# Per-head sums in the projection loop of a four-layer block kernel: four 64x64 products on the four quadrants of TensorE in place of two full products

## The reference, cut to what matters

```python
r, k, v, g, w_lo, a_lo = jnp.split(h, list(np.cumsum(widths)[:-1]), axis=-1)
a = jax.nn.sigmoid(a0 + a_lo @ a2)
...
kk = (k * k_k).astype(jnp.float32)
kk = kk / jnp.maximum(jnp.linalg.norm(kk, axis=-1, keepdims=True), 1e-12)
k = k * (1 + (a - 1) * k_a)
...
bonus = (jnp.sum(r * k * r_k, axis=-1, keepdims=True) * v).reshape(B, L, D_INNER)
```

## Time and profile before

| what | us |
|---|---|
| median of 3 runs (2550.43 to 2552.8) | 2550.72 |
| the profiled execution's own time | 2552.2 |
| its span | 2549.9 |
| TensorE busy | 2213.5 (87%) |
| VectorE busy | 1401.9 (55%) |
| GpSimd busy | 1207.3 (47%) |
| ScalarE busy | 824.4 (32%) |
| mean granted TensorE clock | 0.925 of full speed |

### The profile page before, as it was taken

The page is one execution under the profiler, slowest core; times in us unless marked ns, Lnnn a source line. Parts: engine busy times, 40 slices in busy tenths (PEclk is TensorE's granted clock), DMA queues, the critical chain, the costliest instruction groups (busy, mean ns, idle before and its releaser), DMA issues.

```text
span 2549.9 us, 56210 instructions
## 1 busy us (share of the span) xinstructions
PE 2213.5 (87%) x22038; PEld 1868.7 (73%) x22038; DVE 1401.9 (55%) x2028; ACT 824.4 (32%) x2139; POOL 1207.3 (47%) x708
## 2 busy tenths in 40 slices
PE   6799999988888989886867999999894999798876
PEld 4699989877777878775867976777694776565555
DVE  6766666666666566664445413445415172638655
ACT  1532233325545555453212222333201111211331
POOL 1366656633223132233855831222384897775134
PEclk8899999999988889896987999999897999899998
DMA  2233344372333233323211221000022221221001
GB/s 86 85 141 141 153 150 151 136 196 44 81 62 71 58 71 74 69 48 109 79 64 50 83 74 34 33 33 23 27 83 94 74 91 42 66 83 58 17 0 66
DMA packets 158904, 197.54 MB, mean 77 GB/s; under 512 B 120992, under 2 KB 123296, under 8 KB 156448
## 3 DMA queue, kind: packets, MB, share of 16 engines
q1 hardware_dynamic: 158752, 195.25, 25.2%
HBM read 156.24 MB, written 38.99 MB: 77 GB/s over the span
## 4 chain that ended last, share of the span: by engine, by line
PE 56%; DVE 11%; issue 5%; ACT 4%; POOL 1%; DVEq 1%; ACTq 0%; POOLq 0%
PE wide L797 9%; PE wide L1224 8%; PE wide L1225 8%; PE wide L1226 8%; PE wide L1701 4%; PE wide L1810 2%; PE wide L812 2%; PE wide L820 1%; PE wide L1586 1%; PE wide L1766 1%; DVE x_w L1022 1%; PE wide L814 1%; DVE b_and_k L1015 1%; PE wide L1794 1%; PE wide L2063 1%
## 5 line engine op out<-in xcount | busy, mean ns | idle before, releaser
L1077 POOL TENSOR_TENSOR n_levels<-n,masks 128x192 f32<-128x192 f32 (+1 forms) x96 | 117.8, 1239 | 437.5 <-ACT n L958 437.5
L1224 PE MATMUL wide<-mixed_high,w_high_rwkv_in 128*128 128x264 f32 x720 | 213.0, 296 | 27.8 <-ACT log_decay L435 18.9
L1226 PE MATMUL wide<-mixed_high,w_low_rwkv_in 128*128 128x264 f32 x720 | 207.5, 288 | 0.0
L1341 DVE TENSOR_TENSOR sq_sum<-sq_sum,squares 128x528 f32<-128x528 f32 (+1 forms) x54 | 87.3, 1617 | 178.6 <-ACT squares L1306 178.6
L1225 PE MATMUL wide<-u_low_second,w_high 128*128 128x512 f32 x464 | 185.5, 400 | 0.0
L1248 POOL TENSOR_TENSOR w_high<-weights,con 128x1024 fp32r<-128x1024 f32 x60 | 147.5, 2459 | 73.6 <-PE wide L1226 63.7
L355 PE MATMUL wide<-mixed_in,weights 128*128 128x264 f32 x672 | 158.7, 394 | 13.7 <-DVE mixed_in L325 12.3
L1224 PEld LDWEIGHTS wide<-mixed_high,w_high_rwkv_in 128*128 128x128 f32 x720 | 139.0, 193 | 36.2 <-ACT log_decay L435 25.1
L1251 POOL TENSOR_TENSOR w_low<-weights,w_high 128x1024 fp32r<-128x1024 f32 x60 | 157.6, 2627 | 4.7
L355 PEld LDWEIGHTS wide<-mixed_in,weights 128*128 128x128 f32 x672 | 128.9, 193 | 41.0 <-issue 9.5
L797 PE MATMUL wide<-x_w,n_levels 64*64 64x64 f32 x2752 | 121.8, 231 | 37.8 <-DVE x_w L1022 21.0
(11 more groups left out here) (325 smaller groups left out, 6495.0 us busy)
## 6 DMA issues: line engine op xcount, KB each, us to landing
weights<-in_stream SPq DMA_DIRECT2D x200, 512.0 KB, 3.3
forms<-form SPq DMA_DIRECT2D x16, 2020.5 KB, 6.3
forms_in<-forms SPq DMA_DIRECT2D x96, 144.0 KB, 4.5
forms_in<-forms SPq DMA_DIRECT2D x32, 288.0 KB, 4.5
gate_bonus<-forms SPq DMA_DIRECT2D x16, 576.0 KB, 4.0
r_ahat_r<-forms SPq DMA_DIRECT2D x32, 144.0 KB, 3.1
mixed<-gate_bonus SPq DMA_DIRECT2D x14, 264.0 KB, 2.1
gated<-mixed SPq DMA_DIRECT2D x14, 264.0 KB, 4.8
```

The source lines that it names most:

```text
L1077: return pool.tensor_tensor(n_lvl[:, first:last, grp(g), :], n_all[:, grp(g), :].unsqueeze(1).to_broadcast([P, n, GC, C]), b_con[:, 1 + fi ...
L1224: pe.matmul(dst, w[0], x[0], start=start, stop=False)
L1226: return pe.matmul(dst, w[1], x[0], start=False, stop=stop)
```

## The change

Each sum is made by four products instead of two. Product (head, b) reads the head's 64 rows of half b and writes 64 rows of bank b: for b = 0 the head's own rows, for b = 1 the other head's rows. Each of the four so has its own quadrant of the array. The two readers, ScalarE's square root (line 446) and VectorE's bonus product (line 518), become three instructions each: one for the first half on all 128 partitions, and one per head for the second half, which reads the other head's rows of PSUM and writes the head's rows of SBUF. Ahead of each sum TensorE increments a semaphore `sums_turn` that nobody waits for, so that its waits are taken there, and the two products of head 0 increment `sums_first`, which the readers wait for in addition.

```diff
+        TWO = (slice(0, C), slice(C, P))
+
+        def head_sums(pe, dst, src):
+
+            pe.sem_inc(s["sums_turn"], 1)
+            for hd, rows in enumerate(TWO):
+                for b in range(2):
+                    mm = pe.matmul(dst[TWO[hd ^ b], b, 0:HALF], heads[rows, hd * C:(hd + 1) * C], src[rows, PAD + b * HALF:PAD + (b + 1) * HALF],
+                                   start=True, stop=True)
+                    if hd == 0:
+                        mm.then_inc(s["sums_first"], 1)
+            return mm
+
+        def summed_parts(src):
+
+            cols = [slice(PAD + b * HALF, PAD + (b + 1) * HALF) for b in range(2)]
+            return [(slice(0, P), cols[0], src[:, 0, 0:HALF])] + [(TWO[hd], cols[1], src[TWO[1 - hd], 1, 0:HALF]) for hd in range(2)]
...
             pe.wait_ge(s["k_copied"], i + 1)
             pe.wait_ge(s["kk_squared"], i + 1)
-            for b in range(2):
-                mm = pe.matmul(wide[2][:, b, 0:HALF], heads, a_sq[:, PAD + b * HALF:PAD + (b + 1) * HALF], start=True, stop=True)
-            mm.then_inc(s["kk_summed"], 1)
+            head_sums(pe, wide[2], a_sq).then_inc(s["kk_summed"], 1)
...
-            for b in range(2):
-                mm = pe.matmul(wide[3][:, b, 0:HALF], heads, a_rk[:, PAD + b * HALF:PAD + (b + 1) * HALF], start=True, stop=True)
-            mm.then_inc(s["rk_summed"], 1)
+            head_sums(pe, wide[3], a_rk).then_inc(s["rk_summed"], 1)
...
             act.wait_ge(s["kk_summed"], i + 1)
-            act.activation(real(a_inv), wide[2][:, :, 0:HALF], ACT.Sqrt).then_inc(s["kk_rooted"], 1)
+            act.wait_ge(s["sums_first"], 4 * i + 2)
+            for rows, cols, part in summed_parts(wide[2]):
+                ins = act.activation(a_inv[rows, cols], part, ACT.Sqrt)
+            ins.then_inc(s["kk_rooted"], 1)
...
             dve.wait_ge(s["rk_summed"], i + 1)
-            step(dve.tensor_tensor(real(f_bon), wide[3][:, :, 0:HALF], real(f_v), ALU.mult))
+            dve.wait_ge(s["sums_first"], 4 * i + 4)
+            for rows, cols, part in summed_parts(wide[3]):
+                ins = dve.tensor_tensor(f_bon[rows, cols], part, f_v[rows, cols], ALU.mult)
+            step(ins)
```

More of the change, by code:

```diff
@@ L278, in program @@
             "diff", "lerp", "lora_loaded", "lora_low", "proj_w", "proj_a", "tanh_w", "tanh_a", "k_copied", "r_copied", "kk_squared",
-            "p_exp", "kk_summed", "kk_rooted", "v_copied", "g_tanh", "pc_copied", "rk_summed", "dve", "pool", "stored", "in_rounded", "in_rest", "in_whole")}
+            "p_exp", "kk_summed", "kk_rooted", "v_copied", "g_tanh", "pc_copied", "rk_summed", "dve", "pool", "stored", "in_rounded", "in_rest", "in_whole", "sums_first", "sums_turn")}
         def half_bias(n, pair):
```

## The result

| | changed | before, same chip |
|---|---|---|
| median of the runs | 2575.18 us (2573.42 to 2576.63) | 2551.76 us (2550.43 to 2553.3) |
| ratio | 1.0091, interval 1.0074 to 1.0109 | |
| profiled execution | 2574.58 us, span 2572.8 | 2552.2 us, span 2549.9 |

The change costs 0.9%, 23.4 us of the medians. The forecast was 2556.0 with a range to 2565.5. Both are missed, on the side that rival A was on.

A forecast was written before the change was run, and what follows sets the result against it. TensorE bounds the pair with VectorE 0.18 us behind; VectorE's +0.43 overtakes it. Pairs 3 to 15, 3.1, pair 2, 0.4, pair 0, 1.0, end, 0.8: +5.3 us, 2556.0 against the 2550.72 median; range 2552.0 to 2565.5.

The forecast's parts named there:

- rival A: VectorE's line 500 comes after GpSimd's line 534 and waits it out: +0.91 us per pair, 2565.2 us in all, chance 0.18.
- ScalarE's part: Square root of the sum in three instructions takes 0.95 us in place of 0.61: +0.34, bounds +0.2 to +0.6.
- the point of decision: ScalarE delay, over 0.55 us in place of the forecast 0.34, at which VectorE's line 500 must wait out GpSimd's line 534.
- VectorE's part: Bonus product in three instructions, one every 0.35 us, against 0.62 before: +0.43, bounds +0.3 and +0.6.
- what would show it: The prediction's list of signs in the trace, among them line 500 over 2 us long in all pairs for rival A.
- the slot: Time for VectorE's line 500 ahead of GpSimd's line 534; missing it ends VectorE's chain 0.67 us later than forecast.
- entry and exit as priced: TensorE's cost of changing from the full array to quadrants and back, per sum: 0.15 us in, 0.20 us out.
- The slack of 0.18: Per pair, how far VectorE's chain, ending at line 521, could slip before TensorE's receptance projection is delayed: 0.18 us.
- the 0.21 us to the weight load: Time from the end of VectorE's line 521 to the receptance projection's first weight load: 0.21 us, between 0 and 0.25.
- The gap between two GpSimd instructions: VectorE's line 500 runs between GpSimd's lines 531 and 534; issued at 275.08, before 275.29, it hides ScalarE's 0.34 us.
- The ends: Loop's first and last pairs: pair 0 +0.98 us, line 500 locked out by GpSimd; last chain +0.77 us, both delays counting.
- the forecast's premise: In the readers' three parts, each instruction overlaps the one before, starting 0.10 us before its end on ScalarE.

The follow-up runs named there:

- both_overlapping: Kernel before with both readers in three instructions on all 128 rows, the second half made twice, once into a spare tensor: 28.867 us per pair, ratio 1.0032.
- both_in_three: Kernel before, full products kept, with both readers in three instructions, the short ones on each head's own rows: 29.215 us per pair, ratio 1.0040.
- bonus_earlier_before: Kernel before with VectorE's bonus product, in one instruction, moved ahead of line 510's wait for GpSimd: 28.640 us per pair, ratio 1.0001.
- quadrants_alone: Changed kernel with both readers in one instruction again, the four products and both semaphores kept: 28.479 us per pair, ratio 0.9991.
- the repair: Changed kernel with ScalarE's square-root table loaded early and the bonus product moved ahead of line 527: 28.453 us per pair, ratio 1.0001, repeated 0.9999.
- both_crossed: Kernel before, full products kept, with both readers in three instructions, the short ones reading the other head's rows: 29.940 us per pair, ratio 1.0078.
- root_in_three: Kernel before with only ScalarE's square root in three instructions, the short ones on each head's own rows: 28.640 us per pair, ratio 1.0009.

## Why the prediction was wrong, step by step

**The step that failed** is in ScalarE's part: "An instruction behind another starts 0.10 before that one ends". The row that it came from (line 450 behind line 448) has both instructions start on row 0. Parts that start on other rows than the instruction before them lose this overlap: the root parts came 0.40 apart from start to start in place of 0.28. Two steps make +0.24 more, so the root costs +0.57 in place of +0.34. With some 0.05 from the table load, which now comes behind the sum, the maximum is 0.62 later. The prediction itself put the point of decision at 0.55. The prediction's "part costs known to some 0.05" was false for the same reason: 0.57 lay inside my own bound of +0.6, but beyond the point, so the bound should have moved far more than 0.18 of the chance to rival A.

**VectorE's part** failed by the same step: +0.73 for the bonus in place of +0.43, beyond the bound of +0.6. The two-part row that I used has both instructions on row 0 too.

**Rival A** is what happened: line 517 is long in the steady pairs (2.65 us), as "what would show it" described, and 1.30 per pair in place of its +0.91. The difference is +0.30 from the bonus and 0.1 in the slot. The slot itself cost 0.78 (the mean chain behind the copy of value, 15.46 against 14.36 in both_overlapping, less 0.32 for the bonus) where A had 0.67. The working of A also took 275.22 for GpSimd's issue where the earlier trace rows have 275.29. With that A would have said 0.74 for the slot and +0.98 per pair, some 2566, just outside the range that the prediction gave. The slot is that little for a 2.65 us instruction because line 527 behind it falls out of GpSimd's way: 0.76 us, against 2.67 in both_in_three.

**Right, and confirmed.** TensorE sets the pace before (bonus_earlier_before). Four quadrants side by side, entry and exit as priced, 0.09 per sum (the changed trace, quadrants_alone, 28.453 in the repair). The slack of 0.18 and the 0.21 us to the weight load. The gap between two GpSimd instructions and its threshold. The sum of the steps for a steady pair: +0.24 forecast, +0.23 measured in both_overlapping. Its ratio of 1.0032 on 2550.72 is 2558.9, inside the range, but in part by luck: its loop grew by 2.8 us, and the other 5 lie outside it. Of the Trainium skill, the rule of the page SBUF — State Buffer ("SBUF: two separate sides"), that the first of the two engines keeps the shared port pair for its whole instruction, agrees with every run here (in steady pairs a maximum of 2.57 to 2.70 us where it is issued 0.01 to 0.08 behind GpSimd's instruction, of 0.43 to 0.44 where it is 0.06 to 0.12 ahead). What the Trainium skill's page TensorEngine Tiling (Array Packing) says in Gotcha 1, that different row tiles cannot use one bank at once, doesn't hold for these products: by it the sum would take 0.89, 1.05 with its tails, and the eight records took 0.68 with theirs.

**The ends.** The last pair's chain was forecast at +0.77 and came to 1.35 (0.62 + 0.73), again the same step. Pair 0 was forecast at +0.98 and came to +0.65 (58.18 between the first two key copies, 57.53 before), with the maximum locked out as forecast (2.11 us). This distance lay between 56.1 and 58.2 in all kernels, and in both_overlapping, which has the forecast's premise, it came to +0.05, so the +0.98 is not confirmed.

## What to carry to other kernels
A sum of durations ahead of a threshold, here the gap between two GpSimd instructions, is only as good as its distance to it: where a cost's own bound reaches over the threshold, the step behind it belongs into the forecast. Splitting a reader by partitions costs more than its columns say, since here each part on other rows than the one before started only at that one's end. And take the overlap of instructions from a row whose operands move in the same way as the new ones do.

## What the runs showed of the hardware that I had not expected
On ScalarE a 264-column square root of 0.39 us lets the next one start 0.27 to 0.29 us behind its own start when that one begins on the same rows, and 0.38 to 0.40 behind, 0.01 after its end, when it begins on other rows, on the read or on the written side (where only one side moved the part was also a crossed one, see above). On VectorE the same is 0.34 against 0.43 to 0.45 at 0.42 to 0.43 us each. How many rows a part covers makes no such difference: a part of 64 rows that starts on row 0 behind one of 128 overlaps as one of 128 does (0.286 against 0.287), and so does one of 128 behind one of 64 (0.35 against 0.34, on VectorE). And 0.13 us on ScalarE with 0.11 on VectorE moved a pair by 0.72 us (both_in_three against both_crossed), where a maximum issued 0.45 us later behind the copy of value moved it by nothing (root_in_three against before: 3.01 us behind that copy in place of 2.56).
